# A two-layer hybrid diffusion block in fp32: the first layer's inputs, tables and first readout in another order

## The reference, cut to what matters

```
for l in range(2):
    h = rms_norm(x, ln1) * (1 + scale) + shift          # scale, shift: silu(c) @ ada_w + ada_b
    z = h @ w_in                                        # 512 latent and 256 context tokens
    o_attn = latent_attention(q, k, v)                  # q and k, v through low-rank norms
    o_f = fourier_mix(zf)                               # DFT over positions and channels
    a_bar, b_bar = exp(dt * a), (a_bar - 1) / a * b     # state space: tables from parameters
    s = scan(a_bar, b_bar @ u); o_s = glu(gelu(Re(C s) + D u))
    x = x + g1 * (sum of sigmoid(h @ w_gate) * (o @ w_branch)) @ w_out
    x = x + g2 * square(relu(h2 @ w_mlp1)) @ w_mlp2
```

## Time and profile before

| | |
|---|---|
| median of 3 runs | 2271.76 us (2269.6 to 2276.96) |
| profiled execution | 2277.59 us, its span 2275.8 us |
| PE busy | 2207.1 us of the span |
| DVE, ACT, POOL busy | 1184.1, 505.5, 896.4 us |
| first product of layer 0 | 65.43 us after the span's start |
| first gate tile ends | about 217.7 us |
| first readout starts | about 312.7 us |

### The profile page before, as it was taken

One profiled execution on the slowest core, in us unless ns is written; L12 is line 12 of the kernel. 1 busy time (PEld: TensorE's weight loads), 2 busy tenths in 40 slices (PEclk: granted clock), 3 DMA queues, 4 the chain that ended last, 5 costly groups with the idle time before them and its releaser, 6 DMA issues.

```text
span 2275.8 us, 30561 instructions
## 1 busy us (share of the span) xinstructions
PE 2207.1 (97%) x12500; PEld 1796.8 (79%) x12500; DVE 1184.1 (52%) x1863; ACT 505.5 (22%) x798; POOL 896.4 (39%) x492
## 2 busy tenths in 40 slices
PE   5899999999999999999999999999999999999998
PEld 4688888866678878888888887878876687888886
DVE  5879952046655264334564525484157665552453
ACT  2232122145520131010110212222245312010111
POOL 2223233410034433344443443346421255766663
PEclk9999999999999999999999999999999999999999
DMA  7153343242273313333223232634510344323231
GB/s 283 47 137 94 120 138 108 107 143 81 75 262 135 139 62 114 124 121 114 84 79 107 84 139 109 172 134 142 175 58 22 127 150 150 111 93 102 93 99 68
DMA packets 105697, 267.46 MB, mean 118 GB/s; under 512 B 23136, under 2 KB 42976, under 8 KB 103776
## 3 DMA queue, kind: packets, MB, share of 16 engines
q1 hardware_dynamic: 68352, 187.72, 24.1%
q10 hardware_dynamic: 37216, 77.87, 10.4%
HBM read 227.68 MB, written 37.88 MB: 117 GB/s over the span
## 4 chain that ended last, share of the span: by engine, by line
PE 79%; DVE 10%; DMA 2%; ACT 1%; issue 1%; POOL 0%; ACTq 0%; DVEq 0%; POOLq 0%
PE ps L435 60%; PE ps L954 3%; PE ps L826 3%; PE ps L969 2%; PE ps L997 2%; PE ps L538 2%; DVE terms L1748 2%; DVE terms L1745 2%; PE ps L444 1%; DVE ss L1751 1%; PE ps L864 1%; PE ps L897 1%; DVE t_out L1982 1%; PE ps L450 1%; DMA zs_d<-zs 1%; DMA raw<-in_w_main 1%
## 5 line engine op out<-in xcount | busy, mean ns | idle before, releaser
L1175 POOL TENSOR_SCALAR whi<-raw 128x1024 fp32r<-128x1024 f32 x244 | 270.3, 1108 | 1326.9 <-PE ps L435 665.7
L1178 POOL TENSOR_TENSOR wlo<-raw,whi 128x1024 fp32r<-128x1024 f32 x244 | 626.7, 2569 | 20.3
L435 PE MATMUL ps<-hh,whi 128*128 128x512 f32 (+1 forms) x1560 | 467.9, 356 | 0.3 <-DVE ada L564 0.3
L435 PE MATMUL ps<-hh,wlo 128*128 128x512 f32 (+1 forms) x1560 | 463.7, 354 | 0.0
L435 PE MATMUL ps<-hl,whi 128*128 128x512 f32 (+1 forms) x1560 | 462.6, 353 | 0.0
L435 PEld LDWEIGHTS ps<-hh,whi 128*128 128x128 f32 x1560 | 255.0, 188 | 46.1 <-ACT mr L1549 2.3
L435 PEld LDWEIGHTS ps<-hl,whi 128*128 128x128 f32 x1560 | 255.0, 188 | 44.0 <-issue 0.2
L435 PEld LDWEIGHTS ps<-hh,wlo 128*128 128x128 f32 x1560 | 254.1, 188 | 42.8
L1915 DVE SCALAR_TENSOR_TENSOR x<-ps,ada,x 128x512 f32<-128x512 f32 x120 | 75.5, 659 | 355.5 <-PE ps L435 355.4
L435 PE MATMUL ps<-midh,whi 128*128 128x512 f32 (+1 forms) x768 | 234.3, 359 | 2.6 <-DVE midl L1945 2.6
L435 PE MATMUL ps<-midh,wlo 128*128 128x512 f32 (+1 forms) x768 | 231.9, 356 | 0.0
(11 more groups left out here) (235 smaller groups left out, 2877.2 us busy)
## 6 DMA issues: line engine op xcount, KB each, us to landing
raw<-in_w_main SPq DMA_DIRECT2D x244, 512.0 KB, 3.3
ada_mixer<-in_ada_w SPq DMA_DIRECT2D x32, 512.0 KB, 4.0
ada_gap<-in_ada_w SPq DMA_DIRECT2D x24, 512.0 KB, 7.9
ada_mlp<-in_ada_w SPq DMA_DIRECT2D x24, 512.0 KB, 4.6
g_d<-gt ACTq DMA_DIRECT2D x24, 384.0 KB, 2.3
gl<-g_d ACTq DMA_DIRECT2D x8, 1152.0 KB, 6.0
ada_first<-in_ada_w SPq DMA_DIRECT2D x16, 512.0 KB, 19.0
cout_d<-cz SPq DMA_DIRECT2D x12, 512.0 KB, 5.0
```

The costliest lines, as they stand in the source:

```text
L435: ins = pe.matmul(ps[:, p % 4, a:b], ww[:, w % W_SLOTS, kw * P:(kw + 1) * P], xx[:, kx, a:b], start=(first and i == 0 and j == 0), stop=(l ...
L1175: pool.tensor_scalar(whi[:, u, :], raw[:, u % 2, :], 1.0, 0.0, ALU.mult, ALU.add).then_inc(w_split.sem, 1)
L1178: pool.tensor_tensor(wlo[:, u, :], raw[:, u % 2, :], whi[:, u, :].bitcast(F32), ALU.subtract).then_inc(w_split.sem, 1)
```

## The change

The order of layer 0 is written anew; layer 1's stays but for a few names. Parts:

- SP loads x first (ACT did), then 4 modulation tiles, 2 weight tiles, 12 modulation tiles. ACT's first six loads are the state-space a and b, cvec, ident, ada_b and ln; the other constants and c are loaded behind the norm, on `consts_in`, and ada_b and ln have a semaphore of their own (`mods_in`).
- The squares of x are added on DVE (`add_squares`), as in the later norms, and PE sums only two pieces. Between the squares stand ACT's exponents, sines and silu, and between them DVE's first powers.
- No table is built before the first product. The inverses, the weights and input table 0 stand behind the copies of tiles 0 and 1, the other tables behind tile 2's copy, and all output tables before the scan. PE's transposes stand behind tiles 3 to 7, the kernels behind tiles 8, 10 and 11, and the chunk inputs behind tile 11.
- `cz` has three buffers, one of them in the place of `ss`. DVE and ACT wait for its last store before they write `ss`.
- The scan runs 32 steps, then the folds, 24 steps, the two norm scalings, and 40 steps. In `slots`, the first readout stands behind 15 gate tiles in place of 8 (the argument `before` is 16, it was 9), and the load of cout four slots ahead of it.

```diff
-    before, between = ((9, 5), (16, 5))[l]
+    before, between = 16, 5
...
-FIRST_STORES = {8: (("out", 0), ("out", 1)), 9: (("kernel", 0), ("out", 2)), 10: (("kernel", 1), ("out", 3)),
-                11: (("kernel", 2),), 12: (("kernel", 3), ("out", 4), ("out", 5)), 14: (("kernel", 4), ("kernel", 5))}
+FIRST_STORES = {12: (("out", 0), ("out", 1)), 13: (("out", 2),),
+                15: (("kernel", 0), ("kernel", 1), ("out", 3), ("out", 4)),
+                16: (("kernel", 2), ("kernel", 3), ("out", 5)), 17: (("kernel", 4), ("kernel", 5))}
+IN_PAIRS = ((0, 1, 2, 0, 1, 2, 0, 1, 2, 0, 1, 0), (0, 1, 2, 0, 1, 2, 0, 1, 2, 3, 0, 1))
+FIRST_GATE = (1, 3)
 
 
...
+        L0.cz = [rest(f"cz0{j}", o, [P, 2, SG, CH + 2, GP]) for j, o in enumerate((55296, 60416, 75776))]
...
+            for i in range(2):
+                wait_w(pe, t0 + i)
             if l == 0:
+                for k, steps in ((0, range(8, 11)), (1, range(11, 14))):
+                    first_tiles(range(2), k)
+                    for s in steps:
+                        pe_ada(pe, s)
+                pe.wait_ge(hi_ready.sem, hi_ready.at((0, 1, 2)))
+                for i in range(2):
+                    high_step(pe, i, i, 2, TOK)
+                pe_ada(pe, 14)
+                pe_ada(pe, 15)
+                pe.wait_ge(lo_ready.sem, lo_ready.at((0, 1, 2)))
+                for i in range(2):
+                    low_step(pe, i, i, 2, TOK)
+                pe_turn(pe, 1)
+                for k in range(3, KD):
+                    first_tiles(range(2), k)
+                pe.wait_ge(ada_ready.sem, ada_ready.at(1))
+                tile(2, 2)
+                pe.wait_ge(in_dve.sem, in_dve.at((0, 0)))
+                tile(3, 0)
+                halves(0)
+                pe.wait_ge(in_dve.sem, in_dve.at((0, 1)))
+                tile(4, 1)
+                halves(1)
+                pe.wait_ge(in_dve.sem, in_dve.at((0, 2)))
+                tile(5, 2)
+                halves(2)
+                pe.wait_ge(in_act.sem, in_act.at((0, 3)))
+                square_sums(1, KKV, TOK)
+                pe.wait_ge(sn_root.sem, sn_root.at((0, 1)))
+                tile(6, 0)
+                halves(3)
```

The rest of PE's layer 0, the start on PE, SP and ACT, and DVE's parts:

```diff
+                pe.wait_ge(in_act.sem, in_act.at((0, 5)))
+                halves(4)
+                pe.wait_ge(in_act.sem, in_act.at((0, 4)))
+                tile(7, 1)
+                halves(5)
+                pe.wait_ge(prep_act.sem, prep_act.at((0, "bin", 9)))
+                tile(8, 2)
+                pe.wait_ge(prep_act.sem, prep_act.at((0, "bin", 11)))
+                pe_kernels(pe, 0, 0)
+                pe_kernels(pe, 0, 1)
+                pe.wait_ge(in_act.sem, in_act.at((0, 6)))
+                tile(9, 0)
+                pe.wait_ge(in_act.sem, in_act.at((0, 7)))
+                tile(10, 1)
                 pe_kernels(pe, 0, 2)
...
                 pe_kernels(pe, 0, 3)
...
-            if l == 0:
+                pe.wait_ge(in_act.sem, in_act.at((0, 9)))
+                tile(11, 0)
                 pe_kernels(pe, 0, 4)
                 pe_kernels(pe, 0, 5)
-            pe.wait_ge(in_act.sem, in_act.at((l, 9)))
-            tile(GATES, 3)
-            if l == 0:
+                pe.wait_ge(us_in.sem, us_in.at((0, CH - 1)))
+                pe.wait_ge(in_act.sem, in_act.at((0, 8)))
+                chunk_inputs(0)
                 pe.wait_ge(prep_act.sem, prep_act.at((0, "v", 5)))
...
+            pe_sums(pe, (0, 1), TOK)
+            for s in range(2, 5):
+                pe_ada(pe, s)
+            pe_spread(pe, (0, 1), TOK)
+            for s in range(5, 8):
+                pe_ada(pe, s)
             pe_turn(pe, 0)
-            for h in range(4):
-                pe_half(pe, 0, h)
...
-            for step in range(KD):
+            for j in range(4):
+                sp.dma_start(x[:, 2 * j:2 * j + 2, :], A["x_t"][:, 2 * j:2 * j + 2, :]).then_inc(
+                    x_part[j].sem, x_part[j].mark(0, 16))
+            for step in range(KD // 2):
                 load_ada(step)
             load_w(0)
             load_w(1)
-            for step in range(KD, 2 * KD):
+            for step in range(KD // 2, 2 * KD):
                 load_ada(step)
             for t in range(2, n_all):
                 load_w(t)
...
+            for dst, name in ((ada_b, "ada_b"), (ln, "ln")):
+                act.dma_start(dst[:], A[name]).then_inc(mods_in.sem, mods_in.mark(0, 16))
+            act.wait_ge(ones_ready.sem, ones_ready.at(1))
+            step_sizes(act, 0)
+            act_square(act, (0, 1), TOK, 0)
+            act_square(act, (0, 1), TOK, 1)
+            magnitudes(act, 0)
+            act_square(act, (0, 1), TOK, 2)
+            act_square(act, (0, 1), TOK, 3)
+            sines(act, 0)
+            act_square(act, (0, 1), TOK, 4)
+            act_square(act, (0, 1), TOK, 5)
             act.wait_ge(cvec_in.sem, cvec_in.at(0))
-            act.wait_ge(ones_ready.sem, ones_ready.at("svec"))
             act.activation(svec[:, :, 0:2], cvec[:], ACT.Silu).then_inc(silu_ready.sem, silu_ready.mark(0))
-            exponents(act, 0)
-            act_squares(act, (0, 1), TOK)
+            act_square(act, (0, 1), TOK, 6)
+            act_square(act, (0, 1), TOK, 7)
             act_root(act, (0, 1), TOK)
             act_rows(act, 0)
-            for h in range(4):
...
-                input_tables(dve, 0, 2)
                 dve_ada(dve, 1)
                 dve_gain(dve, 0, 0, KD // 2, KD)
                 dve_norm(dve, 0, 1, TOK, KD // 2, KD)
-                input_tables(dve, 0, 3)
                 inputs(0)
                 inputs(1)
-                input_tables(dve, 0, 4)
+                inverses(dve, 0)
+                input_weights(dve, 0)
+                table_rows(dve, 0)
+                input_tables(dve, 0, 0)
                 inputs(2)
-                input_tables(dve, 0, 5)
+                for c in range(1, S5_PARTS):
+                    input_tables(dve, 0, c)
+                dve.wait_ge(consts_in.sem, consts_in.at(0))
+                dve.tensor_scalar(b_gate[:], b_gate[:], 0.5, None, ALU.mult).then_inc(
+                    ada_ready.sem, ada_ready.mark("gate"))
                 spread_inputs(dve, 0)
-                for c in range(3):
+                for c in range(S5_PARTS):
                     output_tables(dve, 0, c)
+                dve.wait_ge(c_stored[2].sem, c_stored[2].at((0, 5)))
...
+            if l == 0:
+                steps(0, SCAN_FOLD[0])
+            else:
+                steps(0, SCAN_NORM)
+                scale(1, zkv, rs_s, KKV, TOK)
+                steps(SCAN_NORM, SCAN_SPLIT)
+                scale(0, zq, rs_q, KQ, n)
+                steps(SCAN_SPLIT, SCAN_FOLD[1])
             ends()
             for i in range(3):
                 fold(i)
-            steps(SCAN_FOLD, SCAN_EARLY)
-            steps(SCAN_EARLY, NC)
+            if l == 0:
+                steps(SCAN_FOLD[0], SCAN_LATE)
+                scale(1, zkv, rs_s, KKV, TOK)
+                scale(0, zq, rs_q, KQ, n)
+                steps(SCAN_LATE, NC)
+            else:
+                steps(SCAN_FOLD[1], NC)
```

More of the change, by code:

```diff
@@ L327, in build @@
         bin_stored = signal("bin_stored")
-        c_stored = [signal(f"c_stored{j}") for j in range(2)]
+        c_stored = [signal(f"c_stored{j}") for j in range(3)]
         v_stored = [signal(f"v_stored{j}") for j in range(2)]
@@ L1324, in act_layer @@
                 act_kernels(act, 0, 4)
                 act_kernels(act, 0, 5)
-            evacuate(11, zf[:, 2], 1)
+                act.wait_ge(c_stored[2].sem, c_stored[2].at((0, 5)))
+                for q in range(6):
+                    chunk_inputs(q)
+                load_transforms()
+            else:
+                store_inputs()
+                evacuate(3, zkv[:, 0], 0)
+                load_inputs()
+                evacuate(4, zkv[:, 1], 1)
+                act.wait_ge(in_act.sem, in_act.at((l, 4)))
+                for k in range(KKV):
+                    square(1, zkv, k, TOK)
+                key_root()
+                shared_key()
+                for q in range(6):
+                    chunk_inputs(q)
+                load_transforms()
+                for k in range(2):
+                    query_part(k)
+                    query_square(k)
+                query_part(2)
+                for i in range(3):
+                    evacuate(9 + i, zf[:, i], IN_PAIRS[1][9 + i])
@@ L1367, in act_layer @@
                 ins.then_inc(fr_odd.sem, fr_odd.mark((l, i)))
[L1368 to L1370 removed]
+            if l:
+                act.wait_ge(sn_scale.sem, sn_scale.at((l, 0)))
+                for j in range(3):
+                    load_outputs(j)
             v = ss[:].rearrange("p j r g -> p j (r g)")
@@ L1433, in act_layer @@
                 p = TURN[s % 4]
+                if l == 0 and s == y0 - 4:
+                    act.wait_ge(sn_scale.sem, sn_scale.at((l, 0)))
+                    for j in range(3):
```

(1 more changed line is left out.)

377 lines of the change are left out of this document (182 added, 195 removed).

## The result

The changed kernel takes 2257.2 us (median of 4 runs, 2256.0 to 2260.5) against 2274.0 (4 runs, 2269.6 to 2277.0): a ratio of 0.993, 95% interval 0.9916 to 0.9944, and 16.8 us less. Forecast were 22.9 less. The time itself came out 8.3 us above the forecast 2248.9: 3.6 of them are the terms (19.3 for 22.9), and 4.7 come from the step from the profiled execution to the median, for which 5.8 us had been taken off and which is 1.1 in the changed kernel.

The account below looks back on a forecast made before the run. PE was taken as the bound, busy 2207.1 of 2275.8 us. Terms of -27.9, -6.7, +12.8 and -1.1 sum to -22.9 against the profiled 2277.6; with the median 5.8 lower, 2248.9 was forecast, range 2235 to 2265.

Parts of the forecast that it names:

- Term 1: Kernel start: the first product comes at 37.5 us instead of 65.4, minus 27.9 us.
- The sentence on the load order: Kernel start: were x to land late, at about 17, ACT's chain ends some 1 us later, gain about 27.
- Term 2: First product to start of tile 2: 2.5, 3.4 and 0.8 us saved, minus 6.7; tile 2 at 62.2.
- the fourth k hides most of that wait: Behind the second turn: the fourth k covers most of PE's 2.87 us wait; stretch 10.7 us, before 14.1.
- Term 3: Tile 2 to the first gate's end: new waits and half clock give back 12.8 us; gate ends at 195.9.
- The wait for table 0: First transposes: PE asks at 79.4, input table 0 is ready at 82.8; wait 4.5 with half a hold more.
- The wait for kernel 1: Behind tile 8: DVE needs 23.8 us up to two output tables, PE has 20.7; wait 3.1 us.
- the tables are the bound: Rival, tile 3 to chunk inputs: late tables cause 3 more waits, 14 us back, 2263; chance 0.12.
- the last store: Before the first gate's end: the wait for the last store of cz costs 0.5 us.
- Term 4: First readout: toep is in at 328, PE arrives at 348, so the 1.1 us wait goes, minus 1.1.
- the 15 that I had named as the bound: Prediction is wrong if PE waits more than 15 us in all between 62 and 196.
- The scan rival: Rival, first readout: a longer scan makes PE wait; at 60 us more 2266 + 22 = 2288; chance 0.05.

## Why the prediction was right, point by point

**Term 1, the start: right, 28.0 for 27.9, and in part by luck.** The squares ran from 10.0 to 20.7 and didn't wait for PE. Parts were off and made up for each other. PE's sums ended at 26.5, not 23.7: I had counted one sum of 2.7 us, but PE sums two pieces, one behind the other, and the first waits for DVE's last addition (21.1). So the root was ready at 26.8, not 24. diag was ready at 29.5, not 27, since DVE's small operations stand ahead of the inversion and met two splits (2.32 us each); by the root alone it would have been about 28 (an estimate, root plus inversion and diag). In return the spread took 2.3 us for 2.8, and the three modulation tiles behind it ran at full clock, 1.5 us for my 3.2. The sentence on the load order was wrong: I reckoned a loss of 1 us for an x that lands late, since the last squares would still wait; but the chain on ACT begins with the first piece, and that was 3.4 us later, and with the splits that now met DVE's sums the first product 5.6. By the Trainium skill (DMA: Bandwidth & Descriptors, Rules for kernel authors) spreading transfers over the issuing engines brings no bandwidth. The runs agree: from 12 to 22 us it is 409 GB/s with x on SP's queue and 417 with x on ACT's. What the head of a queue brings is an earlier first piece.

**Term 2, the first two tiles: 4.6 for 6.7.** The step "the fourth k hides most of that wait" held (0.6 of wait is left of 2.87). What I had at nothing were the splits of tiles 2 and 3, which hold DVE's first `hl` and cost PE a wait of 1.3 and a longer stretch at half clock. In the profiled executions of five kernels above with the same code up to there, tile 2 stood at 61.3 to 62.4: PE went on to `hl` without that wait, since the split of tile 2 began as the first `hl` was nearly or wholly through. So this term is 4.6 or 7, by where a load lands against that operation; no run sets this on purpose.

**Term 3: +16.0 for +12.8, right in mechanism, too small in two of its sizes.** Both waits stood where they were forecast, with the clock at 0.51 and 0.52 behind them. *The wait for table 0* was 8.0, not 4.5. By dates DVE began its copies 2.7 later (64.05 for 61.4), had more holds (2.2 and 1.4 less the 1.2 that I had added), and PE asked 1.6 later. But the late tile 2 is not a cause: where it starts at 61.4 to 62.4 (the runs with the readout at gate 9, the kernels later and the fourth pair early) the wait is 8.0 as well, since DVE waits 1.5 us for PE's last product of the first two tiles before it copies, and both move together. Counted from the start of tile 2, DVE began 0.15 us ahead of it and not 0.8, had 2.4 more of holds, and PE asked 0.4 sooner: 3.5 in all. Holding the splits back (0.8 of wait left) shows that the holds are its cause, and moving the pair shows that it is one of place. *The wait for kernel 1* was 5.6, not 3.1: table 5 began 1.1 us after the end of tile 6, behind the pair of transposes that frees its buffer, which I had left out, and the holds up to output table 1 cost 7.7 us, not 6.6. Here the rival "the tables are the bound" is half right: from 132.6 on DVE has no gap in the first five output tables, and the runs got rid of this wait by an earlier start only. The other parts came out smaller, as forecast or less: the root 1.0 (1.3), the half clock 3.7 and 5.8 us long, 4.6 lost (5.4), no wait for the last store (0.5). With these sizes the term's sum is 17.2; where the 1.2 us to the measured 16.0 are is not traced.

The rule of the Trainium skill (TensorE: Matmul & The Clock Gate, Why this matters for your kernels), that idle gaps bring the half rate back, was to cost 5.4 here and cost 4.6. Behind the waits of 0.6 and 1.0 us no fall was seen; in the run with the splits held, the wait of 0.8 left the clock at 1.00 and the one of 3.5 was followed by 0.63 over 4.6 us.

**Term 4: right.** The wait of 1.1 for toep is gone. The reserve was smaller than forecast: toep was in at 344.9 (337.67 and 7.2), 10.7 us ahead of the readout, not 20:

```profile
L1899 DVE COPY snat<-ss x1: 3422/3422/3422, 325.9 to 325.9; 64x3072 f32<-64x3072 f32 x1
...
337.67 0.33 ACTq L1482 DMA_DIRECT2D toep<-toep_d  x1
...
355.56 1.03 PE L910 MATMUL ps<-snat,cout 128*128 128x96 f32 x8
```

The scan took 133.0 from the chunk inputs' end at 192.8, not 129, and ACT could copy and issue toep only between gates. Without the seven gates the wait is 30.8, not 38; most likely because the splits stop with PE.

**The sum**: -28.0 - 4.6 + 16.0 - 1.1 - 1.7 behind the first gate elsewhere, most of it the second layer's waits for `us` and a split: -19.3, up to rounding. Half of the -1.7 is chance, since the wait for `us` is 0 to 4.4 from one execution to the next; the late tile 2 of Term 2 is chance the other way, 2.4. PE's waits between 62 and 196 were 14.6 in all, just under the 15 that I had named as the bound. The scan rival's price of "2266 + 22" has no source in the rows; 60 us more of scan is a wait of 40, and 2248.9 + 40 gives the same 2289.

## What to carry to other kernels

When work is taken off the front of a kernel, look for what was hidden under it: of the 32.6 us won up to tile 2, 16.0 came back before the first gate's end, most of it as waits for tables that the old, slow start had covered. A wait for a table is first a question of place: ask for it one tile later, or free its buffer one tile sooner, and look how far the producer's list has slack; where the list has no gap, only its start can be moved. And a number that only sets an order (the gate behind which the readout stands) can be worth more than the change itself: without it this change would be 15 us slower than before.

## What the runs showed of the hardware

A `TENSOR_TENSOR` of 128x1024 on GpSimd holds the DVE operation between SBUF tiles that begins beside it up to its own end, whatever that operation's size: 0.18 us became 2.26. The `TENSOR_SCALAR` of 1.05 us that goes before it does the same (0.40 became 1.20). The 17 operations of the inverses took 3.8 us alone and 11.4 with three splits beside them, 2.5 for a split. An operation already under way as the split begins isn't held (`a`, 0.18 at 68.84). The copy of a power row (L2193, 64x384) was held as well, 2.43 for 0.35; `nt`, which reads PSUM and one tile of SBUF, took its 1.14 for two in every row of this norm, also beside a `TENSOR_SCALAR` of GpSimd (41.17). The Trainium skill (SBUF — State Buffer, SBUF: two separate sides) has the rule: the ports that the two share are an exclusive lock, not a split of bandwidth, and the engine that comes second waits for the whole instruction; for DVE it names operations with two inputs from SBUF or in a mode that uses both ports. The traces agree, with these numbers.

The same code differs from one execution to the next: by where a split begins, tile 2 stood at 64.2 or near 62, and the wait for the load of `us` in the second layer was between 0 and 4.4 us. Differences under 3 us between single executions of this kernel say nothing.
